# A hybrid decoder layer on eight cores: attention steps taken in pairs, VectorE tasks placed by a running account, the last output tiles moved ahead

## The reference, cut to what matters

```python
h = rms_norm(x, norm_w) * (1 + scale) + shift
u_a, v_a, z_a, q_b, k_b, v_b, z_b = split(h @ w_in)
a_out = gmlp(u_a, v_a) * silu(z_a)                      # u_a * (causal mix of rms_norm(v_a) + bias)
q, k  = rope(rms_norm(q_b)), rope(rms_norm(k_b))         # 4 heads, each with 2 components of width 64
p     = softmax(causal(q k^T / 8))                       # per head and component c
o     = (p[c=0] - lam * p[c=1]) @ v_b                    # 4 heads x 128
b_out = rms_norm(o, per head) * subln_w * silu(z_b)
out   = x + gate * (concat(a_out, b_out) @ w_out)
```

## Time and profile before

| | |
|---|---|
| median of 3 runs | 525.61 us (525.59 to 526.62) |
| profiled execution, its own time | 526.04 us |
| its span on the slowest core (core 4) | 524.6 us; the cores lie between 514.8 and 524.6 us |
| busy over the span | TensorE 85%, VectorE 64%, ScalarE 57%, GpSimd 17% |
| first exponential, last group's copy | starts at 276.10 us, at 490.15 us |
| mean granted TensorE clock by core | 0.950 to 0.974 |

### The profile page before, as it was taken

The page is one execution under the profiler, slowest core; times in us unless marked ns, Lnnn a source line. Parts: engine busy times, 40 slices in busy tenths (PEclk is TensorE's granted clock), DMA queues, the critical chain, the costliest instruction groups (busy, mean ns, idle before and its releaser), DMA issues.

```text
span 524.6 us, 9798 instructions; the slowest of 8 cores (514.8 to 524.6 us)
## 1 busy us (share of the span) xinstructions
PE 445.6 (85%) x3104; PEld 217.6 (41%) x3104; DVE 334.7 (64%) x761; ACT 299.2 (57%) x402; POOL 88.6 (17%) x118
## 2 busy tenths in 40 slices
PE   0037679899999999999998999979997999999396
PEld 0002224344443444444445555445554555555242
DVE  1246732682775468888873767788558757868732
ACT  1066456545554227777767666666778778677100
POOL 1113440000671000000001112222222222122100
PEclk9997869899999999999999999979998999999879
DMA  8999978007624300021021122194140131011013
GB/s 200 251 308 257 311 240 180 0 1 131 167 87 139 121 1 2 1 47 36 1 81 41 42 81 60 62 282 202 47 156 2 39 100 67 22 62 42 40 63 139
DMA packets 15606, 53.90 MB, mean 103 GB/s; under 512 B 2242, under 2 KB 2626, under 8 KB 14660
## 3 DMA queue, kind: packets, MB, share of 16 engines
q1 hardware_dynamic: 13924, 45.36, 26.0%
q0 software_dynamic: 1152, 7.50, 8.3%
q10 hardware_dynamic: 480, 0.41, 0.3%
HBM read 50.29 MB, written 8.39 MB: 112 GB/s over the span
## 4 chain that ended last, share of the span: by engine, by line
PE 60%; DVE 11%; DMA 9%; issue 7%; ACT 6%; POOL 5%; DVEq 0%; SPq 0%; ACTq 0%; POOLq 0%
PE psum L647 15%; PE psum L470 13%; PE psum L1049 8%; PE psum L927 7%; DMA sb_WO<-w_adaT 5%; PE psum L897 5%; ACT sb_cs L910 3%; DMA sb_kT<-xT 3%; PE psum L1015 3%; POOL sb_cs L915 3%; DVE sb_F L984 3%; DVE sb_F L943 1%; PE psum L677 1%; PE psum L675 1%; PE psum L667 1%
## 5 line engine op out<-in xcount | busy, mean ns | idle before, releaser
L910 ACT ACTIVATE sb_cs<-psum,sb_small 128x1024 bf16<-128x1024 f32 x144 | 150.9, 1113 | 58.6 <-PE psum L897 55.2
L927 PE MATMUL psum<-sb_vB,sb_cs 128*128 128x129 bf16 x1088 | 89.5, 226 | 9.7 <-DVE sb_F L943 5.2
L927 PEld LDWEIGHTS psum<-sb_vB,sb_cs 128*128 128x128 bf16 x1088 | 64.4, 100 | 40.5 <-issue 40.1
L470 PE MATMUL psum<-sb_W,sb_hT 128*128 128x512 bf16 x256 | 65.8, 420 | 17.5 <-ACT sb_hT L466 15.4
L915 POOL TENSOR_TENSOR sb_cs<-sb_cs,sb_constb 128x256 bf16<-128x256 bf16 x64 | 44.5, 697 | 213.3 <-ACT sb_cs L910 208.7
L647 PE MATMUL psum<-sb_hT,sb_W 128*128 128x512 bf16 x280 | 65.8, 379 | 0.0
L897 PE MATMUL psum<-sb_qT,sb_kT 64*128 64x256 bf16 (+1 forms) x576 | 56.4, 274 | 6.9 <-ACT sb_cs L910 4.7
L470 PEld LDWEIGHTS psum<-sb_W,sb_hT 128*128 128x128 bf16 x256 | 26.4, 105 | 56.2 <-issue 34.1
L357 DVE SCALAR_TENSOR_TENSOR sb_F<-sb_WO,sb_F 128x1024 f32<-128x1024 f32 x24 | 30.2, 1257 | 30.5 <-DMA sb_WO<-w_adaT 22.0
L647 PEld LDWEIGHTS psum<-sb_hT,sb_W 128*128 128x128 bf16 x280 | 27.3, 98 | 30.0
L436 PE MATMUL psum<-sb_vnA,sb_constb 128*128 128x512 bf16 x32 | 11.9, 507 | 30.5 <-ACT sb_vnA L429 30.5
(11 more groups left out here) (114 smaller groups left out, 548.4 us busy)
## 6 DMA issues: line engine op xcount, KB each, us to landing
sb_WO<-w_adaT SPq DMA_DIRECT2D x24, 512.0 KB, 8.1
sb_W<-w_in POOLq DMA_DIRECT2D x5, 1024.0 KB, 9.9
sb_W<-x SPq DMA_DIRECT2D x8, 512.0 KB, 4.4
sb_cs<-w_out SPq DMA_DIRECT2D x8, 512.0 KB, 3.4
sb_hT<-x SPq DMA_DIRECT2D x8, 512.0 KB, 12.0
...
```

What stands on the lines that cost most here:

```text
L470: pe(lambda E: E.matmul(PS(bank), lhsT=hT[:, kc, 128 * tt:128 * (tt + 1)], rhs=wsl[slot][:, kc, :], start=(kc == 0), stop=(kc == KC - 1)), ...
L910: act(lambda E: E.activation(out=et, in_=psum[:, X:X + 2, :], func=AF.Exp, bias=negM, scale=0.125), reads=[pb[X], pb[Y], b_lam], writes=[b ...
L927: pe(lambda E, u=u, j=j, c=c, i=i: E.matmul(psum[:, j, 256 * c:256 * c + 129], lhsT=et[:, c, QB * u + 128 * j:QB * u + 128 * (j + 1)], rhs ...
```

## The change

Five things change in the second part.

1. The loop takes steps in pairs. TensorE gets QK, QK of the next pair, then matmuls of fill, then PV, PV of this pair; where the pair's first step ends a group, the fill comes between the two PV.
2. Fill goes matmul by matmul, 4.8 per pair on average (2 more in a pair whose first step ends a group), so tiles are spread over pairs.
3. `group_end` copies only component 0 of both banks, in one instruction; the reciprocals and the two multiply-adds read component 1 and the sums from PSUM.
4. VectorE's tasks have costs; a running account of TensorE's and VectorE's time (`tpe`, `tdv`) lets a task go only if it ends ahead of the next group's end, or if more than 6 wait. The norm's last multiplication comes two steps after its ScalarE part. The u buffers grow from 3 to 4; the raw and square scratch are single.
5. Behind the loop all output tiles that are left of earlier blocks come ahead of the last block's transposes, and 6 banks are used in place of 2.

```diff
-        for j in range(2):
-            dve(lambda E, j=j: E.tensor_copy(out=raw[a][:, j, :, 0:129], in_=O4[:, j, :, 0:129]),
-                reads=[pb[j]], writes=[b_rw[a][j]])
-        dve(lambda E: E.reciprocal(out=rc[b][:, h], in_=raw[a][:, :, :, 128]), reads=b_rw[a], writes=[b_rc[b][h]])
+        dve(lambda E: E.tensor_copy(out=raw[a][:, :, 0:129], in_=O4[:, :, 0, 0:129]), reads=pb[0:2], writes=b_rw[a])
+        dve(lambda E: E.reciprocal(out=rc[b][:, h], in_=O4[:, :, :, 128]), reads=pb[0:2], writes=[b_rc[b][h]])
...
-                out=uu[b][:, j, h, :], in0=raw[a][:, j, 1, 0:128], scalar=snl[a][:, j:j + 1], in1=raw[a][:, j, 0, 0:128],
-                op0=ALU.mult, op1=ALU.add), reads=[b_rw[a][j], b_snl[a]], writes=[b_uu[b][h]])
+                out=uu[b][:, j, h, :], in0=O4[:, j, 1, 0:128], scalar=snl[a][:, j:j + 1], in1=raw[a][:, j, 0:128],
+                op0=ALU.mult, op1=ALU.add), reads=[pb[j], b_snl[a]] + b_rw[a], writes=[b_uu[b][h]])
...
             if h == 3:
-                later(now[0] + (3 if now[0] < NS else 0), lambda: block_norm(jq))
-        taskq.append(squares)
+                later(now[0] + 3, lambda: block_norm(jq))
+                later(now[0] + 5, lambda: taskq.append((0.3, lambda: norm_scale(jq))))
+        taskq.append((1.1, squares))
...
+    def tasks(limit, force=99):
+        while taskq or lowq:
+            if taskq:
+                cost, fn = taskq[0]
+                if max(tdv[0], tpe[0]) + cost > limit and len(taskq) <= force:
+                    return
+                taskq.pop(0)
...
+    for p in range(NP):
+        g0, g1 = 2 * p, 2 * p + 1
+        now[0] = g0
+        e0 = do_exp(g0)
+        e1 = do_exp(g1)
+        if p + 1 < NP:
+            do_qk(g0 + 2)
+            do_qk(g0 + 3)
+        quota += 4.8
+        ends0 = gsteps[g0][4]
+        n = int(quota) + (2 if ends0 else 0)
+        quota -= n
+        if not ends0:
+            fill(n)
+        do_pv(g0, *e0)
+        tpe[0] += 0.55 + 0.48 + (0 if ends0 else 0.216 * n)
+        close(g0)
+        if ends0:
+            fill(n)
+            tpe[0] += 0.216 * n
+        do_pv(g1, *e1)
+        tpe[0] += 0.48
+        close(g1)
+        dv(0.75 * len(posts))
         run_posts()
-        run_due(gs)
-        if not last or len(taskq) > 5:
...
-        if (last or (gs > 0 and jq >= 6 and kp == 3)) and fillq and len(posts) < 2:
-            fill_one()
+        run_due(g1)
+        tasks(next_end(g1 + 1), 6)
+    now[0] = NS
+    FB[0] = [2, 3, 4, 5, 6, 7]
...
+    trs = [fillq.pop(0)]
+    assert trs[0][0] == "tr" and (not fillq or fillq[0][0] != "tr")
+    fill(8 * 5)
+    fillq.insert(0, trs[0])
     s = NS + 1
...
+        run_due(s)
+        fill(16)
         s += 1
```

More of the change, by code:

```diff
@@ L1043, in out_tile, with mm @@
         cc = slice(512 * half, 512 * (half + 1))
-        for m in range(KC):
+        def mm(m):
             if m < 4:
@@ L1060, in post @@
                     x_load(k + NX - 2)
-        return post
+        return [lambda m=m: mm(m) for m in range(KC)], post
     fillq = []
@@ L1109, in _build_body @@
     now = [0]
+    cur = []
     def run_posts():
-        for fn in posts:
+        for bank, fn in posts:
             fn()
@@ new lines, in fill @@
+    def fill(n):
+        while n > 0 and (cur or fillq):
+            if not cur:
+                open_tile()
+            kind, mms, bank, post = cur[0]
+            if kind == "tr":
+                n += 1
+            while mms and n > 0:
+                mms.pop(0)()
+                n -= 1
+            if not mms:
+                cur.pop()
+                posts.append((bank, post))
+                if kind == "u":
+                    u_left[0] -= 1
+                    if u_left[0] == 0:
+                        b_xr[2].inherit([b_w[0]])
+                        b_xr[3].inherit([b_w[0]])
+                        for i in range(4, NX):
+                            b_xr[i].inherit([x for tb in range(TB) for x in b_h[tb]])
+                        for k in range(2, NX):
+                            x_load(k)
@@ L1179, in _build_body @@
+    now[0] = NS
+    FB[0] = [2, 3, 4, 5, 6, 7]
+    fb_ctr[0] = 2 if fb_ctr[0] % 2 == 0 else 3
+    assert not lowq
+    while taskq or due:
+        while taskq:
+            taskq.pop(0)[1]()
+        if fillq and fillq[0][0] == "tr":
+            break
+        run_due(10 ** 9)
+    trs = [fillq.pop(0)]
+    assert trs[0][0] == "tr" and (not fillq or fillq[0][0] != "tr")
+    fill(8 * 5)
+    fillq.insert(0, trs[0])
     s = NS + 1
-    while due or fillq or posts or taskq:
+    assert not taskq
@@ L1181, in _build_body @@
+    while due or fillq or posts or cur:
         now[0] = s
         run_posts()
-        while taskq:
-            taskq.pop(0)()
-            run_due(s)
         run_due(s)
-        for k in range(2):
-            if len(posts) < 2 and fillq:
-                fill_one()
+        fill(16)
         s += 1
```

136 lines of the change are left out of this document (73 added, 63 removed).

## The result

The changed kernel takes 549.95 us (median of 4 runs, 547.39 to 551.59) against 525.6: ratio 1.046, 95% interval 1.040 to 1.051. Forecast was 501, with 489 to 514 as range.

A forecast was written before the change was run, and what follows sets the result against it. TensorE and ScalarE were taken to bound the loop in turns, with TensorE idle, then slow-clocked, in the tail. Loop -13 and tail -11 sum to -24 us, giving 501 us from 525.61, range 489 to 514.

The forecast's parts named there:

- The ScalarE part of a norm: In the loop: ScalarE's norm work waits for VectorE's squares ahead of exponentials, 2.5 us in all, taken as unchanged.
- The w_out tasks priced at nothing: In the loop: w_out tasks move with VectorE's posts and cost nothing; a late one would only hold the first output tiles.
- The clock term: In the loop: 5 us added, between 0 and 12, for the account's misjudged group ends and stretches of lower clock.
- My mark: Sign of being wrong: the loop's granted clock, 0.97 before, falls under 0.93.
- 174.8 of TensorE's own work and 26 added: Loop sum: 174.8 us of TensorE work, plus 10 for ScalarE, 11 for held banks, 5 for account and clock.
- The bank hold: At 32 group ends: PV waits 0.35 us each for multiply-adds to free banks 0 and 1, 11 us, within 5 to 27.
- slower by the same place: Rival: the hold ends in VectorE's queue; beyond 0.75 us lateness per group end the kernel is slower; chance 0.04.
- TensorE's own work and ScalarE's chain: In the loop: a pair takes TensorE 1.55 us plus fill; ScalarE's chain holds pairs with thin fill to about 2.5.
- The tail: From the last group's copy to the end: 23.1 us against 34.45, so -11, with TensorE resting 2.6.
- What it had only as an "if": In the tail: if the rest of 2.6 us brings the low clock, some 2 us come back.
- The loop's gain of 13: In the loop: steps in pairs and the other edits bring 214 us to 201, a gain of 13.
- The noise: What the measurement can tell from no change: about 0.2%, 1 us.

The follow-up runs named there:

- e1_norm: The changed kernel with each block's norm two steps (one pair) later; ratio 1.028 to the kernel before.
- e16_early: The kernel before with a block's norm one step after its group's end in place of three; ratio 1.028 to the kernel before.
- e3_both: The changed kernel with the norm two steps (one pair) later and w_out tasks at least two pairs apart; ratio 1.014 to the kernel before.
- e13_norm7: e3_both with the norm seven steps after the group's end in place of five, its scaling at nine; ratio 1.009 to the kernel before.
- e4_tail: The kernel before with only the new end: five output tiles ahead of the last transposes, six banks; ratio 0.985 to the kernel before.
- e15_norm7_copies: e13_norm7 with the old two copies of both components out of PSUM ahead of the combination; ratio 0.999 to the kernel before.
- e17_tr: e15_norm7_copies with a block's transposes one pair later, four steps after the last scaling task in place of two; ratio 1.000 to the kernel before.
- e14_norm9: e3_both with the norm nine steps after the group's end in place of five, its scaling at eleven; ratio 1.018 to the kernel before.

## Why the prediction was wrong

- **The step that failed** is "The ScalarE part of a norm still stands ahead of exponentials and waits for squares; that was 2.5 us over the loop and stays". It did not stay: it became 18.2 us. I carried a wait over from a trace though the change moved both its ends: three steps had been three iterations of VectorE's tasks and became one pair's. Putting it right gives back 1.8% (e1_norm), and e16_early, the kernel before with this one number changed, has the same waits (18.6) and loses 2.8%.
- **The w_out tasks priced at nothing** was the second. I looked at who needs the result and not at what the tasks wait for: 4.6 us of waits for data before, 16 us after, with a group's end queued behind. It cost 1.4%, measured with the norm mended (e1_norm to e3_both).
- **The clock term** ("For this and for stretches of lower clock ... I add 5") was mis-sized, and it is where the larger part of the two stalls' price was paid: an estimated 20 us at the low clock, 6 before and 5 in e3_both. My mark, a loop clock under 0.93, was met with 0.90. In the forecast's terms the loop was 174.8 of TensorE's own work and 26 added; measured it is some 185 of work, 20 of slow clock and 46 not busy (before: 190, 6 and 18).
- **The bank hold**, 0.35 x 32 = 11 us, within 5 to 27: PE waited 23.1 us after, but 6.96 of it in one w_out stall. With stalls mended it waited 18.1 (e13_norm7) against 5.8 with copies, and the whole cost was 1.0%, some 5 us. My rival "slower by the same place" named the right row, and the wrong reason: the lateness came from two outside waits, not from VectorE's sum of work, which was 136.6 us and so no bound, as I had it (140).
- **TensorE's own work and ScalarE's chain** held where nothing stalled: score runs at 277.20, 279.62, 282.40, 284.98 and 287.55 are 2.4 to 2.8 us apart for a forecast of 2.5 to 2.63, and two multiply-adds from PSUM took 0.81 us, the same as two from SBUF. The cost table of the Trainium skill, "VectorE: DVE Perf Modes", section "The TRN2 errata — SBUF-src ops pay a fixed extra latency per instruction", puts 62 cycles more on a PSUM source; these rows do not show them. The advice of its section "Rules for kernel authors", to copy first where many operations follow, paid here for another reason: the banks that stay taken (1.0% between e13_norm7 and e15_norm7_copies).
- **The tail** was right in size and steps: 24.2 against 22.7, a rest of 2.62 for a forecast of 2.6, two waits of 2.2 for transfers. What it had only as an "if" came, the low clock behind that rest. e4_tail shows the new end alone, -10.
- **The loop's gain of 13** does not exist even when mended. e15_norm7_copies and e17_tr, with norm, w_out, copies and transposes put right, are level with before though the new end is worth 1.5% alone; if the two simply add, their loop costs 1 to 1.5% of the time more than the old one. Their TensorE is busy 188 to 189 us where it was 197, so the work saved is real, and it is not busy for 31 to 35 us where it was 18. Nearly all of this is waits for other engines: 30 us in e17_tr's loop (score banks 9.5, output tiles' banks 10.1, PV 5.6, transposes 3.7, others 1.4) against 16.3 before (45 in after). Whether an order in pairs can do without them is open; e14_norm9 and e17_tr with their longer leads moved work into the tail and won nothing.
- **The noise** was put too low, at 0.2%: the ratio's interval is half a per cent to either side.
